# Filler products on TensorE ahead of its waits at the borders of stages

## What is computed

```python
h = concat(meta_tokens, x)                                    # 528 x 1024
h = h + ssd_mixer(rmsnorm(h, ssd_norm) ...)                   # state-space mixer
h = h + conv_ffn(rmsnorm(h, ffn_norm[0]) ...)                 # "ffn0"
h = h + stick_breaking(rmsnorm(h, ...), rmsnorm(h, ...)) @ w_o # "sb"
h = h + conv_ffn(rmsnorm(h, ffn_norm[1]) ...)                 # "ffn1"
x = rmsnorm(h, final_norm)[16:]                               # 512 tokens from here
x = x + (fox_attention | retention of rms_norm(x)) @ w_out    # "even"
x = x + nsa_attention(rms_norm(x) ...) @ w_out                # "odd"
return rms_norm(x, final_g)                                   # "last"

def rmsnorm(x, g):  return x * rsqrt(mean(x * x, axis=-1) + 1e-6) * g
def conv_ffn(u):    h = causal_conv3(u @ w_up); g, v = split(h); return (silu(g) * v) @ w_down
```

## Time and profile before

| | us |
|---|---|
| median of 3 runs | 2554.26 |
| lowest and highest of them | 2550.91, 2557.08 |
| the profiled execution, its own time | 2552.04 |
| its span in the trace | 2550.3 |
| mean granted clock of TensorE in it | 0.954 |

### The profile page before, as it was taken

How to read it: one execution, slowest core, us unless ns; L and a number is a source line. 1 busy time by engine, 2 the same in 40 slices (tenths; PEclk the granted TensorE clock), 3 DMA queues, 4 the chain that set the end, 5 groups by cost and what they waited for, 6 DMA issues and landing times.

```text
span 2550.3 us, 39242 instructions
## 1 busy us (share of the span) xinstructions
PE 2374.4 (93%) x16208; PEld 2057.0 (81%) x16208; DVE 1259.0 (49%) x1940; ACT 885.2 (35%) x1351; POOL 1008.5 (40%) x977
## 2 busy tenths in 40 slices
PE   7979999887999999999998999998998799989997
PEld 6768878677999999995588989986785478876776
DVE  6455666657861764334448725742113541014553
ACT  4233334324232333335632323332224431225551
POOL 3221323123454553003233555544345433327861
PEclk9889989879999999999998999999998999989999
DMA  3101111101222223220011222222221012520000
GB/s 148 67 34 50 67 50 52 49 34 67 71 87 101 84 83 109 84 83 34 1 50 67 81 94 100 89 85 83 83 103 63 17 67 74 176 100 1 35 2 33
DMA packets 29376, 175.63 MB, mean 69 GB/s; under 512 B 3985, under 2 KB 4497, under 8 KB 12305
## 3 DMA queue, kind: packets, MB, share of 16 engines
q1 hardware_dynamic: 29200, 173.14, 19.3%
HBM read 166.71 MB, written 2.10 MB: 66 GB/s over the span
## 4 chain that ended last, share of the span: by engine, by line
PE 55%; issue 23%; POOL 13%; DVE 3%; POOLq 3%; ACT 1%; SPq 1%; DVEq 1%; DMA 0%; ACTq 0%
PE PS L670 16%; PE PS L671 16%; PE PS L672 16%; POOL ring_r L2306 8%; PE PS L950 2%; POOLq L2414 1%; POOL arena L2378 1%; POOL arena L2413 1%; POOL uT L2417 1%; PE PD L980 1%; POOL uT L2390 1%; PE PC L1201 1%; PE PC L950 1%; DVEq L394 1%; POOLq L2375 1%
## 5 line engine op out<-in xcount | busy, mean ns | idle before, releaser
L2306 POOL TENSOR_TENSOR ring_r<-ring,arena_r 128x512 fp32r<-128x512 f32 (+1 forms) x576 | 763.9, 1357 | 1319.9 <-ACT arena_r L1298 1319.9
L672 PE MATMUL PS<-arena_r,ring_r 128*128 128x264 f32 (+3 forms) x3728 | 1148.2, 308 | 0.0
L672 PEld LDWEIGHTS PS<-arena_r,ring_r 128*128 128x128 f32 x3728 | 718.5, 193 | 31.0
L670 PE MATMUL PS<-arena_r,arena_r 128*128 128x264 f32 (+3 forms) x2288 | 693.5, 303 | 21.8 <-issue 18.7
L671 PE MATMUL PS<-arena_r,arena_r 128*128 128x264 f32 (+2 forms) x2256 | 676.8, 300 | 0.0
L670 PE MATMUL PS<-arena_r 128*128 128x264 f32 (+3 forms) x1792 | 568.6, 317 | 23.5 <-DVEq L394 9.8
L670 PEld LDWEIGHTS PS<-arena_r,arena_r 128*128 128x128 f32 x2288 | 436.1, 191 | 49.9 <-issue 30.5
L671 PE MATMUL PS<-uT_r,arena_r 128*128 128x264 f32 (+2 forms) x1472 | 472.8, 321 | 0.0
L671 PEld LDWEIGHTS PS<-arena_r,arena_r 128*128 128x128 f32 x2256 | 430.5, 191 | 13.8 <-issue 1.2
L1298 ACT ACTIVATE arena_r<-ring 128x2048 fp32r<-128x2048 f32 (+1 forms) x146 | 262.0, 1795 | 435.9 <-PE PS L672 421.0
L670 PEld LDWEIGHTS PS<-arena_r 128*128 128x128 f32 x1792 | 350.8, 196 | 48.9 <-issue 21.0
(11 more groups left out here) (320 smaller groups left out, 2844.4 us busy)
## 6 DMA issues: line engine op xcount, KB each, us to landing
ring<-stream SPq DMA_DIRECT2D x130, 1024.0 KB, 4.8
ring<-down SPq DMA_DIRECT2D x32, 704.0 KB, 4.1
hT<-x_in SPq DMA_DIRECT2D x4, 528.0 KB, 7.2
arena<-tables SPq DMA_DIRECT2D x4, 512.0 KB, 3.8
arena<-arena SPq DMA_DIRECT2D x16, 128.0 KB, 2.4
out<-uT SPq DMA_DIRECT2D x4, 512.0 KB, 2.9
par<-params SPq DMA_DIRECT2D x1, 1634.5 KB, 13.9
arena<-arena SPq DMA_DIRECT2D x8, 136.0 KB, 2.7
```

The costliest lines, as they stand in the source:

```text
L670: mm(out_, r32(ah), r32(bh), start=start, stop=False)
L672: return mm(out_, r32(a), r32(bh), start=False, stop=stop)
L2306: last = G.tensor_tensor(r32(low[:, cut]), raw[:, cut], split(high[:, cut]), ALU.subtract)
```

## The change

A helper `busy(n, bank)` issues n products of `ones` with `causal` (128x512, float32) into a bank of `PD`, with nothing waited for and no semaphore raised. It is called in three places of TensorE's stream:

- in `stats`, ahead of the wait for `total_full`: 4 products in "ffn1", 6 in "even", 4 in "odd", 3 in "last", none in "ffn0" and "sb";
- in `project_units` for the stages "ffn0a" and "ffn1a", ahead of the units r = 1 and r = 2: 4 products each;
- in `odd_transposes(0)`, ahead of its wait for `cp_full`: 8 products into the second bank.

These are 17 + 16 + 8 = 41 products, or 82 recorded instructions. Nothing reads their results, and no other engine's stream changes.

```diff
+            def busy(n, bank=0):
+
+                for _ in range(n):
+                    mm(PD[:, bank, :], ones, prm("causal"), start=True, stop=True)
+
             def stats(name, width, tokens=False):
 
                 pc = PC[:, :, :].rearrange("p a b -> p (a b)")
                 v0 = first_column(width)
+                busy({"ffn1": 4, "even": 6, "odd": 4, "last": 3}.get(name, 0))
                 pe.wait_ge(sem("total_full"), NORM[name] + 1)
...
                 for r in units if isinstance(units, range) else range(units):
+                    if stage in ("ffn0a", "ffn1a") and r in (1, 2):
+                        busy(4)
                     unit_ready(stage, 0, r)
...
                 pe.wait_ge(sem("ns_c0"), f)
+                if n == 0:
+                    busy(8, 1)
                 if ODD[n][0] == "blocks":
                     pe.wait_ge(sem("cp_full"), c + 1)
```

## The result

| | us |
|---|---|
| before, median of 8 runs | 2556.18 (2550.91 to 2560.0) |
| after the change, median of 8 runs | 2545.74 (2544.09 to 2548.64) |
| ratio | 0.9964, 95% interval 0.9953 to 0.9975 |
| the profiled execution of after, its own time and span | 2545.77, 2544.0 |

The change makes the kernel 0.36% faster, 9.2 us of 2555, within 6.4 to 12.0. Two executions in a much slower state, one of e2 at 3623.85 us and one of e3 at 4205.10 us, are left out of all medians and ratios.

What follows compares the result with a forecast made beforehand. TensorE was taken as the bound wherever it isn't waiting at a border; 4.0 + 3.2 + 1.5 + 1.5 - 1.5 + 0 + 0 = 8.7 us off a median of 2554.26 gave 2545.6, with 8 in 10 between 2541.5 and 2554.5.

Steps and rivals of the forecast that it cites:

- Price and fit of the fillers: All filled waits: 0.87 us a product at full clock; those in `stats` fit, overrunning by 0.3 at the upper end.
- "even" 4.0: Border to "even", first sum to T2: 12.96 us would take 8.95 at full clock, 4.0 us saved.
- "odd" 3.2: Border to "odd", sums to T2: 11.31 us would take 8.1 at full clock, 3.2 us saved.
- "ffn1" 1.5: Border to "ffn1", VectorE the bound: 0.9 us from faster sums, 0.63 from its wait for T1, together 1.5 gained.
- T6 of ffn0a, 1.5 lost: Tile T6 of ffn0a: idle time ahead grows from 2.96 to 4.0, the clock falls, 1.5 us lost.
- T6 of ffn1a, 1.5 gained: Tile T6 of ffn1a: idle time ahead shrinks from 3.96 to 3.5, the clock is kept, 1.5 us gained.
- The loop, 0: `odd_transposes(0)`: filler late by 1.5 to 4 us, 2.3 given back; between 0.8 gained and 1.7 lost, taken as 0.
- the clock falls all the same: Rival, all borders: fillers don't count or remaining idle time suffices; all gains go, 2554.3 to 2555.8 us; chance 0.13.
- The filler is late: Rival, borders and loop: fillers begin at half clock and hold up `stats`; 19 us slower, 2573; chance 0.08.
- It moves the idle time: Rival, ffn0a: the filler moves idle time rather than fills it; counted in the sum, no chance of its own.

Runs made afterwards that it cites:

- e2: Kernel before plus only the fillers at r = 1 and 2 of ffn0a and ffn1a: 2559.49 against 2555.0 us, ratio 1.0019.
- e3: Kernel before plus only the 8 products ahead of the odd loop's first transposes: 2553.50 against 2555.0 us, ratio 0.9990.
- e6: The change with fillers ahead of T6 (3 in ffn0a, 4 in ffn1a) replacing those at r = 1 and 2, against before: 2543.31 against 2556.6 us.
- e1: Kernel before plus only the fillers ahead of the sums (4, 6, 4, 3): 2547.42 against 2555.0 us, ratio 0.9969.
- e5: The change plus 4 products ahead of T6 (unit r = 3) in ffn0a and ffn1a, against before: 2538.57 against 2556.6 us, ratio 0.9928.
- e9: The change as it is, run again beside e10, against the kernel before: 2545.91 us, ratio 0.9971.
- e10: The same kernel as e5 on another chip, against the kernel before: 2543.08 against 2554.4 us, ratio 0.9962.
- e4: Kernel before plus only doubled fillers ahead of the sums (8, 12, 8, 6): 2556.24 against 2555.0 us, ratio 1.0003.
- e11: e5 plus 12 products ahead of the first layer's last output projections, 3 in odd's window values, 2 before "sb" sums, against before: 2544.82 against 2554.4 us.
- e8: e5 plus 12 products ahead of the first layer's last output projections and 3 in "od_z", against before: 2542.90 against 2556.6 us, ratio 0.9947.

## Why the prediction was right, and where it wasn't

Forecast 2545.6, measured 2545.74; forecast 8.7 us gained, measured 9.2. The mechanism is right, and so are the three terms that carry the sum; three smaller terms were wrong. That the totals agree so well is luck. By the table, the terms of the sum come to 4.0 + 3.2 + 1.6 - 1.1 - 2.4 + 1.5 = 6.8 us, and all that lies behind the first layer to 7.8. And the median of before, from which I subtracted, rose from 2554.26 with three runs to 2556.18 with eight.

- **Price and fit of the fillers: right.** 0.86 us a product, where I took 0.87; in these runs of the change no sum was held up by as much as 0.1, and the idle time left at the three borders was 0.3 to 0.8 us. The 1.1 us of e6 at "even" is the exception that I had not allowed for: the tile ahead of the filler at half clock.
- **"even" 4.0, "odd" 3.2: right** to 0.1 us in five executions with these fillers (after, e1, e5, e9, e10). The banks were free in time; in "even" VectorE was done with T0 at 1756.43 in the trace after, and T2 started at 1756.86.
- **"ffn1" 1.5: right**, 1.5 to 1.6, by the path forecast: full clock for the sums, and VectorE no longer waiting for T1.
- **T6 of ffn0a, 1.5 lost: right in kind, too small.** The idle time grew to 4.16 (forecast 4.0), and the clock fell. 0.58 over the 7 us from 656 leaves it low until 661.9, which is 5.5 us of T6's products (from 656.44) and not the 3 that I took from T6 of ffn1a. It cost 2.4 us, 2.5 in e2.
- **T6 of ffn1a, 1.5 gained: wrong**, 1.1 lost. The idle time was as forecast, 3.56 against 3.5. The step that failed is "nearer to 3.28, I take it as kept": the clock was lost in both profiled executions of the change, and it then stayed low for longer than before, 5.6 us from T6's start (1386.75) to 1392.3 in place of 3, so the term changed its sign. Over all traces, an idle time of 3.35 and one of 2.57 lost the clock, and 3.28 and 3.17 kept it. The divider between 3.28 and 3.96 did not hold in the trace of before either. I had overlooked a row there, in the attention of "even":

```profile
1964.32 2.07 PE L1098 MATMUL PD<-arena 128*128 128x512 f32 x2 [2.38 <-ACT arena L1555]
```

The two halves of one product of 512 columns took 2.07 us, as at half clock in the earlier trace rows, behind an idle time of 2.38.

TensorE's timeline at the values of "odd", in e9 (lost) and e10 (kept):

```profile
2204.05 0.58 PE L676 MATMUL PS<-arena_r 128*128 128x256 f32 x1 [2.57 <-ACT arena L1453]
...
2202.51 0.39 PE L676 MATMUL PS<-arena_r 128*128 128x256 f32 x1 [2.28 <-ACT arena L1453]
```

The first product at 0.58 us is one at half clock, the 0.39 one at full clock, as in the earlier trace rows. Length is thus a poor divider below 3.5 us; every idle time from 3.5 to 5.5 in these traces lost the clock.

- **The loop, 0: too low.** 1.5 us gained at its start. The term that was mis-sized is how late the filler comes, 1.5 to 4 us in the forecast: in the traces of the change the clock came back just as it began, with the scores ahead of it, and the transposes were not late at all; in e3, e5 and e6 they were 0.5 to 0.7 late. The 2.3 given back behind it were right, 2.2 by 2303, but 0.8 of them were gone again by 2330. Over the rest of the loop it is between 1.6 gained and 1.5 lost, and by e3 the whole is worth 2.6 (0 to 4.9).
- **Not in the sum: stretches with the same code.** The attention of "even" gained 1.9 and the values of "odd" lost 2.3. Neither is shown to be luck. All nine profiled executions whose sums of "even" have 3 or 6 fillers gained 0.8 to 1.9 in that attention, and before, e2, e3 and e4 (none, or 12) differ there by 0.1 at most. Both profiled executions of the change lost 2.1 to 2.3 in the values of "odd", and e1, e5 and e10 did not. What decides it stays open. The profiled execution of before was 4.1 below the median of the eight, so the traces differ by 6.3 in span and the medians by 10.4. I had taken account of 2.2.

Of the rivals, "the clock falls all the same" is refuted by the 1.00 at three borders and by e1: products of ones with a constant mask hold the clock. In the Trainium skill, "TensorE: Matmul & The Clock Gate", section "What's actually happening", it is how busy TensorE has been that sets the clock, with no word of the data; this trace agrees. The section "A second HAM failure mode: psum-queue depth-cycling" of the same page of the Trainium skill, by which short idle pieces are enough to lose the clock, has more to it than I gave it: the clock did fall behind 2.3 and 2.6 us, in "sb" (e5, e10) behind pieces of 1.75, 1.17 and 0.54, and in the attention of "even" behind 0.88 and 1.67. "The filler is late" is the mechanism that e4 shows, at double the length. "It moves the idle time" is what e2 shows for the units, with 2.5 us at T6 of ffn0a, where the sum had 1.5; the 4.9 of its run is more than its trace can place.

What stays open: the additions. e1, e2 and e3 sum to 5.6 us faster, the whole is 9.2 and 7.4 in two batches; each has an interval of 2 to 3 us either way, so no more than rough agreement can be claimed.

## What to carry to other kernels

Fill a wait only where TensorE's own products behind it are late for someone: at a border whose sum or first tiles release the next engine, the borders of "even" and "odd" gave back 4.0 and 3.2 us, about half of their time at half clock, and "ffn1" gave 1.6, which is what VectorE had been waiting for the sums and for T1. Size the filler under the wait, since here every product beyond it cost its full time (e4), and leave some room, since the tile ahead can be slow itself (e6). In a stretch that another engine bounds look where the idle time goes next, for it may come to stand in front of the first tile that matters. Judge single fillers by setting the two traces' products against each other, for a total of one execution has several microseconds of clock luck in it.

## What the runs showed that I had not expected

- Behind idle times of 2.3 to 3.4 us the clock falls in one execution and not in another: 2.31, 2.57, 3.01 and 3.35 lost it, 2.28, 2.90, 3.17 and 3.28 kept it.
- In the attention of "sb", code that is the same in all kernels but e11 lost 0, 1.6 or 3.2 us. The first layer, the same in all but e8 and e11 until its end, differed by up to 5.8 us between executions.
- The low clock behind T6 of ffn0a lasted 5.5 us of dense products; ahead of the change it had lasted 3 in T6 of ffn1a.
